# Sampled attention: the last gate weights in slot 5 of the ring, and the queries' copies and two key transposes inside the prompt's attention heads

## The chip, the cores and the metric

The kernel runs on one core of a Trainium2 chip. A core has TensorE (matrix products, PE), VectorE (DVE), ScalarE (ACT), GpSimd (POOL) and SyncE (SP), which issues most of the transfers; 16 DMA engines move the data. The engines run side by side and wait for one another through semaphores. The metric is the device time of one execution in microseconds; lower is better.

## The reference, cut to what matters

It is one layer of a hybrid decoder for a prompt of 256 tokens and 8 sampled sequences of 4 tokens, all float32. One input projection feeds two token mixers, a gated linear attention (branch A) and a softmax attention with a forget bias (branch B, called FoX, 8 heads of 128), and the branch gates. A mixture of experts follows.

```python
qa, ka, va, ra, lra, qb, kb, vb, fb, ga, gb = jnp.split(h @ w_in, offs, axis=-1)
# prompt: causal attention per head, logit[t,s] += F_t - F_s
s = jnp.einsum('bqhd,bkhd->bhqk', qi, k).astype(jnp.float32) * scale
s = s + fi[..., None] - Ft[:, :, None, :]
# samples: 8 pages of 128 keys per sequence, found through page_table, plus the new tokens
k_past = cache_k[page_table].reshape(DB, -1, H, Dh)
v_past = cache_v[page_table].reshape(DB, -1, H, Dh)
s_past = jnp.einsum('bqhd,bkhd->bhqk', q, k_past).astype(jnp.float32) * scale
# both branches meet through the gates
merged = jax.nn.sigmoid(ga) * u_a + jax.nn.sigmoid(gb) * u_b
```

## The kernel before

There are 288 tokens (256 of the prompt, 32 sampled), kept as columns. All weights and cache pages pass through a ring of six slots of 2 MB (`slot(0)` to `slot(5)`). Every engine has its own program, written by hand in one order, and what sets the order between engines is semaphores: `ring_free{s}` says that slot s may be filled, `ring_full{s}` or `kv_full{s}` that it is filled. Each engine and each queue works strictly in the order of its program, so a wait holds everything that stands behind it.

**The gates.** The gate projection (`ga`, `gb`) is used as filling for TensorE. `gates(count)` in the TensorE program does the next `count` steps of it: one step is one product of a 128x128 block of weights with the 288 tokens, and 16 steps make one gate block j. In the trace a float32 product leaves two records, so two steps are four. There are 24 blocks before the sampled attention. Their weights come in 12 loads of 2 MB, load m for blocks 2m and 2m+1, into slots 0 and 1 in turn; ScalarE copies each finished block to a buffer, and the queue of SP stores it (`store_gate`). Eight more blocks follow later, one per sampled sequence (`late_gate`).

**The prompt's heads.** The loop over i from 0 to 8 does, in turn i, the scores of head i and then the weighing of head i-1: TensorE scores, VectorE adds the mask (L1380) and takes the maxima (L1705), ScalarE exponentiates, VectorE inverts the sums (L1712) and scales the probabilities, TensorE transposes them (L642), VectorE copies, TensorE multiplies with the values, VectorE copies the result. TensorE does `gates(5)` behind the scores of a head and `gates(2)` behind the transposes; turn 8 has only the weighing of head 7, with `gates(2)`. With these, the 384th step (the end of block 23) is the last one of turn 8.

**Between the heads and the sampled attention.** After the heads TensorE scores the new tokens (16 pairs of small products). VectorE masks them (L1380), clears `o_all` (L1746), takes the minimum (L1748), and spreads the queries `qb` over the partitions into `q4` by sixteen copies of 32x256. The K pages of a sequence fill slots 0 (pages 0 to 3) and 1 (pages 4 to 7), its V pages slots 2 and 3. VectorE turns keys in blocks of 32x32 (`turn_keys`, L1736) out of slots 0 and 1 into `kT`. That tile lies in slots 4 and 5: heads 0 to 3 (g = 0) in slot 4, heads 4 to 7 (g = 1) in slot 5. Four transposes make one sequence: g = 0 from slot 0, g = 0 from slot 1, g = 1 from slot 0, g = 1 from slot 1; each of the last two frees its slot for the next sequence. `score(b)` on TensorE needs the first two for its first half and all four for its second.

**Who holds slots 4 and 5.** Until then they are the working memory of branch A (`wk`). Its last reader is GpSimd, which multiplies the output of branch A by its norm (L574), its gain (L576) and, all of it at once, by the output gate (L578), and then signals `oa_final`. Just ahead of these it issues the stores of the new K and V (L565 to L570), and just behind them the loads of the forget sums `r_rep` (L585).

Of the kernel before, what the change touches and what calls it, by code (L numbers as in the profile page):

```python
# [17 lines left out]
P = 128  # L18
D = 2048
KT = D // P  # L20
TP = 256
DB, DT = 8, 4
TS = DB * DT
T = TP + TS
# [48 lines left out]
def build(nc, io, out):  # L73
    with ExitStack() as ctx:
# [208 lines left out]
        def place(n):  # L283

            later = LATER if n >= UP and n % SLOTS < 2 else 0
            return n // SLOTS - (1 if n % SLOTS < 2 else 0) + later
# [20 lines left out]
        def later_place(m):  # L307

            return place(UP + m % 2) - LATER + m // 2
# [5 lines left out]
        def _(sp):  # L315
# [45 lines left out]
            for m in range(12):  # L361
                sp.wait_ge(sem(f"ring_free{m % 2}"), later_place(m) + 1)
                at = (COL_GA, COL_GB)[m // 8] + m % 8 * 256
                sp.dma_start(slot(m % 2).rearrange("p (k n) -> p k n", k=KT),
                             io["w_in"][0, :, at:at + 256].rearrange("(k p) n -> p k n", p=P)).then_inc(sem(f"ring_full{m % 2}"), 16)
                if m >= 2:
                    store_gate(2 * m - 4)
                    store_gate(2 * m - 3)
            def gates_back(g):
# [24 lines left out]
            pages(0, 3, lead(3))  # L394
            store_gate(20)
# [4 lines left out]
            pages(0, 1)  # L400
# [229 lines left out]
        def _(pe):  # L630
# [112 lines left out]
            def gates(count):  # L743

                for _ in range(count):
                    j, k = divmod(len(blocks_done), KT)
                    m = j // 2
                    if k == 0:
                        if j % 2 == 0:
                            pe.wait_ge(sem(f"ring_full{m % 2}"), 16 * (later_place(m) + 1))  # L750
                        if j >= 2:
                            pe.wait_ge(sem("gate_copied"), j - 1)
                    w = slot(m % 2).rearrange("p (k n) -> p k n", k=KT)[:, k, j % 2 * P:(j % 2 + 1) * P]
                    last = mm(ps[:, 7 - j % 2, 0:T], w, hT[:, k, :], k == 0, k == KT - 1)
                    blocks_done.append(last)
                    if k == KT - 1:
                        last.then_inc(sem("gate_tile"), 1)
                        if j % 2 == 1:
                            release("gate_tile", j + 1, m % 2)
# [247 lines left out]
            pe.wait_ge(sem("q4_ready"), 1)  # L1007
# [370 lines left out]
        def _(v):  # L1378
# [316 lines left out]
            v.sem_inc(reach("f_ready"), 1)  # L1695
            for i in range(H_B + 1):
                if i < H_B:
# [29 lines left out]
            v.wait_ge(sem("kv_stored"), 6 * 16)  # L1727
# [13 lines left out]
            v.wait_ge(sem("oa_final"), 1)  # L1741
            turn_keys(0, 0, 1, False)
# [3 lines left out]
            nc.vector.memset(o_all, 0.0)  # L1746
# [4 lines left out]

            for part in range(4):
                for a in range(4):
                    last = copy(q4[32 * a:32 * a + 32, :, part, :], qb[32 * part:32 * part + 32, :, TP:T])
            last.then_inc(sem("q4_ready"), 1)
# [30 lines left out]
            turn_keys(0, 1, 4, False)  # L1786
# [275 lines left out]
```

## Time and profile before

| | |
|---|---|
| timed runs | 1976.27, 1983.96, 1987.64 us; median 1983.96 |
| the profiled execution | 1982.53 us, of which the span from the first to the last instruction is 1980.7 |
| TensorE | 1790.8 us busy, 90% of the span |
| VectorE, ScalarE, GpSimd | 531.5, 209.3, 158.5 us busy |
| DMA | 530.86 MB, 268 GB/s over the span |
| granted TensorE clock | 0.953 of full speed on average |

In rows of the profile, L632 and L642 are the two helpers through which all products and transposes of TensorE go, L1380 to L1389 those of VectorE, L1202 that of ScalarE; the tiles tell which work it is. `ring` is a slot or something kept in one, `hT` the tokens, `z`, `work` and `xT` large working tiles, `ps` the result banks of TensorE. "x4" counts records. In square brackets stands how long the engine had been idle before the row, and what ended it. SPq is the queue of SP with its DMA issues. Times are microseconds from the start of the span.

### The profile page before, as it was taken

The page shows a single profiled execution, that of the slowest core. Times are in us where ns is not written, and L with a number is a line of the kernel's source. Part 1 is how long each engine was busy: PE and PEld are TensorE (multiplying, and loading weights), DVE is VectorE, ACT ScalarE, POOL GpSimd, SP SyncE. Part 2 cuts the span into 40 slices and gives each one's busy share as a digit, 9 for nine tenths or more (in the row PEclk, how much of TensorE's full clock was granted, in tenths as well). Part 3 has the DMA queues.
Part 4 walks back from the last instruction along what each step waited for, and adds up shares of the span by engine and source line. Part 5 has one row for each costly group of instructions (what it writes and reads, how often), then busy time and mean ns, then how long its engine had stood idle before and what let it go on. Part 6 is the DMA issues. An engine that isn't in the chain of part 4 may idle for free.

```text
span 1980.7 us, 28087 instructions
## 1 busy us (share of the span) xinstructions
PE 1790.8 (90%) x11118; PEld 1121.3 (57%) x11118; DVE 531.5 (27%) x1145; ACT 209.3 (11%) x403; POOL 158.5 (8%) x274
## 2 busy tenths in 40 slices
PE   6589999999998999997888999998699898999998
PEld 3145666666666786775766777775333333333334
DVE  2020000000008654436555111002423222232223
ACT  2010000000001110211222100002210001000102
POOL 1011011110201000240000000000100000000000
PEclk9789999999999999998989999999799898998999
DMA  9997766685814433747999883333399999999991
GB/s 357 422 351 289 255 256 251 222 322 180 295 46 140 145 98 108 237 154 243 392 391 359 330 294 138 103 117 139 122 359 408 401 392 386 406 384 396 388 399 48
DMA packets 150459, 530.86 MB, mean 268 GB/s; under 512 B 17702, under 2 KB 61900, under 8 KB 123612
## 3 DMA queue, kind: packets, MB, share of 16 engines
q1 hardware_dynamic: 124980, 432.32, 57.6%
q0 software_dynamic: 17088, 97.15, 14.0%
q10 hardware_dynamic: 8336, 0.66, 0.3%
q8 instruction: 36, 0.59, 0.1%
q14 instruction: 19, 0.15, 0.0%
HBM read 510.94 MB, written 19.15 MB: 268 GB/s over the span
## 4 chain that ended last, share of the span: by engine, by line
PE 75%; DMA 12%; DVE 5%; issue 3%; SPq 3%; DVEq 1%; ACT 1%; POOLq 0%; POOL 0%; ACTq 0%
PE ps L632 73%; DMA ring<-in_w_up_e_dram 4%; DMA xT<-in_w_ada_dram 3%; DMA ring<-in_w_ada_dram 3%; PE ps L642 2%; DMA xT<-in_w_in_dram 1%; SPq L384 1%; SPq L378 1%; DVE z L1389 1%; DVE ring L1386 1%; DVE z L1380 1%; DMA z<-in_x_sample_dram 0%; DVEq L2012 0%; DVE ring L1476 0%; DVE ring L1380 0%
## 5 line engine op out<-in xcount | busy, mean ns | idle before, releaser
L632 PE MATMUL ps<-hT,ring 128*128 128x288 f32 x2304 | 585.7, 411 | 9.5 <-ACT hT L1202 6.0
L632 PEld LDWEIGHTS ps<-hT,ring 128*128 128x128 f32 x2304 | 433.1, 191 | 167.7 <-issue 55.3
L632 PE MATMUL ps<-ring,work 128*64 128x512 f32 (+1 forms) x1280 | 281.6, 642 | 36.1 <-DMA ring<-in_w_ada_dram 24.7
L632 PE MATMUL ps<-z,ring 128*128 128x288 f32 (+1 forms) x1040 | 257.5, 408 | 4.5 <-PE ps L632 2.7
L1389 DVE COPY z<-ps 128x256 f32<-128x256 f32 (+7 forms) x98 | 64.3, 659 | 689.8 <-PE ps L632 669.0
L632 PE MATMUL ps<-ring,z 32*32 32x256 f32 (+3 forms) x3744 | 217.2, 400 | 25.8 <-DVE z L1389 11.1
L632 PEld LDWEIGHTS ps<-z,ring 128*128 128x128 f32 x1040 | 197.8, 191 | 62.3 <-issue 6.1
L632 PEld LDWEIGHTS ps<-ring,work 128*64 128x64 f32 (+1 forms) x1280 | 78.3, 136 | 205.1 <-issue 165.6
L632 PEld LDWEIGHTS ps<-ring,z 32*32 32x32 f32 (+3 forms) x3744 | 108.9, 115 | 122.5 <-issue 115.4
L1202 ACT ACTIVATE z<-ps 128x512 f32<-128x512 f32 (+4 forms) x108 | 60.4, 601 | 922.0 <-PE ps L632 910.1
L1386 DVE SCALAR_TENSOR_TENSOR xT<-ps,modT,xT 128x256 f32<-128x256 f32 x160 | 70.8, 480 | 263.6 <-PE ps L632 263.6
L642 PE MATMUL ps<-ident,z 64*128 64x64 f32 (+4 forms) x644 | 92.6, 289 | 42.1 <-DVE z L1380 28.0
L642 PEld LDWEIGHTS ps<-ident,z 64*128 64x128 f32 (+4 forms) x644 | 76.8, 179 | 65.4 <-issue 47.2
L632 PE MATMUL ps<-z 128*128 128x288 f32 (+3 forms) x408 | 109.8, 394 | 2.5 <-DVEq L2023 1.5
L632 PEld LDWEIGHTS ps<-z 128*128 128x128 f32 (+1 forms) x408 | 64.5, 188 | 71.0 <-DVEq L1993 46.1
L632 PE MATMUL ps<-hT,xT 128*128 128x288 f32 (+1 forms) x352 | 84.8, 402 | 19.2 <-DMA xT<-in_w_in_dram 19.2
L632 PEld LDWEIGHTS ps<-hT,xT 128*128 128x128 f32 (+1 forms) x352 | 64.3, 199 | 39.3 <-DMA xT<-in_w_in_dram 20.9
L632 PE MATMUL ps<-xT,work 128*32 128x512 f32 x512 | 67.3, 617 | 13.0 <-DMA xT<-in_w_ada_dram 13.0
L1736 DVE STREAM_TRANSPOSE ring<-ring 128x2048 f32<-128x2048 f32 x32 | 72.2, 2291 | 5.4 <-issue 3.7
L1202 ACT ACTIVATE work<-ps 128x512 f32<-128x512 f32 (+2 forms) x73 | 35.5, 510 | 354.8 <-PE ps L632 306.3
L522 POOL DMA_DIRECT2D xT<-in_w_ada_dram x64 | 34.5, 538 | 319.5 <-PE ps L632 292.2
L608 POOL COPY rstd<-rstd 64x1 int32 (+1 forms) x17 | 3.2, 187 | 472.9 <-PE ps L642 463.4
(201 smaller groups left out, 822.4 us busy)
## 6 DMA issues: line engine op xcount, KB each, us to landing
ring<-in_w_in_dram SPq DMA_DIRECT2D x36, 2048.0 KB, 12.8
xT<-in_w_ada_dram POOLq DMA_DIRECT2D x64, 1024.0 KB, 7.2
ring<-in_w_gate_e_dram SPq DMA_DIRECT2D x32, 2048.0 KB, 13.4
ring<-in_w_up_e_dram SPq DMA_DIRECT2D x32, 2048.0 KB, 18.7
ring<-in_w_down_e_dram SPq DMA_DIRECT2D x32, 2048.0 KB, 15.4
ring<-in_w_ada_dram SPq DMA_DIRECT2D x16, 2048.0 KB, 26.2
ring<-in_cache_v_dram SPq DMA_DIRECT2D x64, 512.0 KB, 5.9
ring<-in_cache_k_dram SPq DMA_DIRECT2D x64, 512.0 KB, 6.0
```

Source lines behind the costliest of these rows:

```text
L378: pg = sp.value_load(ptab[0:1, ds(b * NPG + (s % 2 * 4 + n), 1)], min_val=0, max_val=io["cache_k"].shape[1] - 1)
L384: sp.dma_start(slot(s)[:, n * 1024:(n + 1) * 1024], io[name][0, ds(pg, 1)].rearrange("a p h d -> (a p) (h d)")).then_inc(sem(f"kv_full{s}" ...
L522: pool.dma_start(late[:, k % 2, :], io["w_ada"][0, k * P:(k + 1) * P, ds(i * D + 2 * D, D)]).then_inc(sem(f"late_full{k % 2}"), 16)
L608: pool.tensor_copy(take, token_i[:, ds(w, 1)])
L632: return nc.tensor.matmul(o, lhsT, rhs, start=start, stop=stop, skip_group_check=free)
L642: return nc.tensor.transpose(o, i, ident[0:n, 0:n])
L1202: return nc.scalar.activation(o, i, func, **kw)
L1380: return nc.vector.tensor_tensor(o, a, b, op)
L1386: return nc.vector.scalar_tensor_tensor(out=o, in0=a, scalar=s, in1=b, op0=op0, op1=op1)
L1389: return nc.vector.tensor_copy(o, a)
L1736: nc.vector.transpose(kT[:, g, 4 * half:4 * half + 4], slot(half).rearrange("p (n g e) -> p n g e", n=4, g=2)[:, :, g]).then_inc(sem("keys ...
```

## The change

Three things change, and no arithmetic among them.

1. The last load of gate weights (m = 11, for blocks 22 and 23) goes to slot 5 instead of slot 1, with a semaphore of its own, `last_gates_full`. It waits for `oa_final`. The second half of the first keys, `pages(0, 1)`, is issued ahead of it.
2. VectorE spreads the queries in turns 5 and 6 of the prompt's heads, and does the first two key transposes in turns 7 and 8. What stood behind the heads loses the sixteen copies and two of the four transposes.
3. Before its last two transposes, which write slot 5, VectorE waits until all 24 gate blocks are done; `o_all` is cleared ahead of the new tokens' mask.

```diff
-            later = LATER if n >= UP and n % SLOTS < 2 else 0
+            later = LATER - n % SLOTS if n >= UP and n % SLOTS < 2 else 0
...
-            for m in range(12):
+            def gate_columns(m):
+                at = (COL_GA, COL_GB)[m // 8] + m % 8 * 256
+                return io["w_in"][0, :, at:at + 256].rearrange("(k p) n -> p k n", p=P)
+
+            for m in range(11):
                 sp.wait_ge(sem(f"ring_free{m % 2}"), later_place(m) + 1)
...
             pages(0, 2, lead(2))
             pages(0, 3, lead(3))
+            store_gate(18)
+            store_gate(19)
+            pages(0, 1)
+            sp.wait_ge(sem("oa_final"), 1)
+            sp.dma_start(slot(5).rearrange("p (k n) -> p k n", k=KT), gate_columns(11)).then_inc(sem("last_gates_full"), 16)
             store_gate(20)
             store_gate(21)
             pages(0, 0)
             store_gate(22)
             store_gate(23)
-            pages(0, 1)
             pages(1, 0)
             pages(1, 1)
...
                     if k == 0:
-                        if j % 2 == 0:
+                        if j == 22:
+                            pe.wait_ge(sem("last_gates_full"), 16)
+                        elif j % 2 == 0:
                             pe.wait_ge(sem(f"ring_full{m % 2}"), 16 * (later_place(m) + 1))
...
-            pe.wait_ge(sem("q4_ready"), 1)
+            pe.wait_ge(sem("q4_ready"), 2)
...
+            def spread_queries(*parts):
+
+                for part in parts:
+                    for a in range(4):
+                        last = copy(q4[32 * a:32 * a + 32, :, part, :], qb[32 * part:32 * part + 32, :, TP:T])
+                last.then_inc(sem("q4_ready"), 1)
+
+            def first_keys(half):
+
+                v.wait_ge(sem(f"kv_full{half}"), 64)
+                nc.vector.transpose(kT[:, 0, 4 * half:4 * half + 4], slot(half).rearrange("p (n g e) -> p n g e", n=4, g=2)[:, :, 0]).then_inc(sem("keys_turned"), 1)
+
             for i in range(H_B + 1):
+                if i == 5:
+                    v.wait_ge(sem("kv_stored"), 6 * 16)
+                    spread_queries(0, 1)
+                if i == 6:
+                    spread_queries(2, 3)
+                if i == 7:
+                    v.wait_ge(sem("oa_final"), 1)
+                    first_keys(1)
+                if i == 8:
+                    first_keys(0)
...
-            v.wait_ge(sem("oa_final"), 1)
-            turn_keys(0, 0, 1, False)
+            nc.vector.memset(o_all, 0.0)
...
-            turn_keys(0, 1, 4, False)
+            v.wait_ge(sem("gate_tile"), 24)
+            turn_keys(0, 2, 4, False)
```

The queue of SP, at the last load of gate weights, before (L364 is a load of gate weights, L359 the stores of gate blocks, L378 and L384 the V pages of the first sequence):

```order
L364 DMA ring<-in_w_in_dram 128x16x256 [waits ring_free1]
L359 DMA gates_kept<-work 128x288 [waits gate_copied] x2
L378 TENSOR_LOAD ptab
L378 ISA x2
L384 ISA [waits ring_free2,dve_step]
L384 DMA ring<-in_cache_v_dram 128x1024
```

And of the change (L402 is now the last load of gate weights, L387 the pages):

```order
L387 DMA ring<-in_cache_k_dram 128x1024
L402 DMA ring<-in_w_in_dram 128x16x256 [waits oa_final]
L359 DMA gates_kept<-work 128x288 [waits gate_copied] x2
L381 TENSOR_LOAD ptab
L381 ISA x2
L387 ISA [waits ring_free0]
L387 DMA ring<-in_cache_k_dram 128x1024
```

The load has moved behind eight V pages, two stores and the four K pages of slot 1, and it waits for GpSimd instead of TensorE; the stores of blocks 20 and 21 and the K pages of slot 0 now stand behind that wait.

TensorE in turn 3 of the prompt's heads, where block 22 begins, before (a transpose of head 2's probabilities, the gate steps, the product with the values, the scores of head 4):

```order
L642 MATMUL ps<-ident,z 128x128 [waits gate_tile,fox_pt,fox_prob]
L642 MATMUL ps<-ident,z 128x128 x2
L632 MATMUL ps<-hT,ring 128x288 [waits gate_copied,ring_full1]
L632 MATMUL ps<-hT,ring 128x288
L632 MATMUL ps<-z 128x128 [waits fox_out,fox_pt]
```

And of the change:

```order
L649 MATMUL ps<-ident,z 128x128 [waits gate_tile,fox_pt,fox_prob]
L649 MATMUL ps<-ident,z 128x128 x2
L639 MATMUL ps<-hT,ring 128x288 [waits gate_copied,last_gates_full]
L639 MATMUL ps<-hT,ring 128x288
L639 MATMUL ps<-z 128x128 [waits fox_out,fox_pt]
```

Nothing moves on TensorE; the first gate step of block 22 waits for the new semaphore, and everything behind it on TensorE stands in line.

VectorE from the last copy of turn 7 to the first copies of the forget sums, before:

```order
L1389 COPY z<-ps 128x256
L1712 RECIPROCAL z<-z 128x2
L1383 TENSOR_SCALAR z<-z 128x128
L1383 TENSOR_SCALAR z<-z 128x256
L1389 COPY z<-ps 128x384
L1389 COPY z<-ps 128x256
L1736 STREAM_TRANSPOSE ring<-ring 128x2048
L1380 TENSOR_TENSOR xT<-ps,new_mask 128x2x32
L1746 MEMSET z 128x256
L1748 TENSOR_REDUCE z<-xT 128x2
L1389 COPY z<-z 32x8x32 x16
L1736 STREAM_TRANSPOSE ring<-ring 128x2048 x3
```

And of the change:

```order
L1398 COPY z<-ps 128x256
L1715 STREAM_TRANSPOSE ring<-ring 128x2048
L1743 RECIPROCAL z<-z 128x2
L1392 TENSOR_SCALAR z<-z 128x128
L1392 TENSOR_SCALAR z<-z 128x256
L1398 COPY z<-ps 128x384
L1398 COPY z<-ps 128x256
L1771 MEMSET z 128x256
L1389 TENSOR_TENSOR xT<-ps,new_mask 128x2x32
L1776 TENSOR_REDUCE z<-xT 128x2
L1766 STREAM_TRANSPOSE ring<-ring 128x2048 x2
```

One transpose now stands ahead of the reciprocal of turn 8, the sixteen copies are gone from here, and two transposes follow the new tokens' minimum where three did. In turns 5, 6 and 7 eight copies, eight copies and one transpose stand in the same place ahead of the mask of the turn's head.

## Rows read from the trace of the kernel before

**Rows 1.** The page: busy time by engine, and the chain's shares.

```profile
PE 1790.8 (90%) x11118; PEld 1121.3 (57%) x11118; DVE 531.5 (27%) x1145; ACT 209.3 (11%) x403; POOL 158.5 (8%) x274
...
PE 75%; DMA 12%; DVE 5%; issue 3%; SPq 3%; DVEq 1%; ACT 1%; POOLq 0%; POOL 0%; ACTq 0%
```

**Rows 2.** Timeline from 870 us: start, length, engine, line, operation.

```profile
887.98 0.55 PE L642 MATMUL ps<-ident,z 128*128 128x128 f32 x3 [1.24 <-DVEq L1717]
...
888.37 1.14 PE L632 MATMUL ps<-hT,ring 128*128 128x288 f32 x4
...
889.54 0.41 ACT L1202 ACTIVATE work<-ps 128x288 f32<-128x288 f32 x1 [5.01 <-PE ps L632]
...
891.09 2.30 DVE L1736 STREAM_TRANSPOSE ring<-ring 128x2048 f32<-128x2048 f32 x1
...
893.87 0.24 PE L632 MATMUL ps<-fT,ident 8*32 8x32 f32 x2
...
894.37 0.27 DVE L1746 MEMSET z<- 128x256 f32 x1
...
895.06 4.76 DVE L1389 COPY z<-z 32x256 f32<-32x256 f32 x16
900.29 6.96 DVE L1736 STREAM_TRANSPOSE ring<-ring 128x2048 f32<-128x2048 f32 x3 [0.47 <-DMA ring<-in_cache_k_dram]
...
902.74 7.48 PE L632 MATMUL ps<-ring,z 32*32 32x256 f32 x241 [8.64 <-DVE ring L1736]
```

**Rows 3.** Timeline of the queue of SP, from 800 us.

```profile
826.50 0.39 SPq L364 DMA_DIRECT2D ring<-in_w_in_dram  x1
...
830.51 10.79 SPq L384 DMA_DIRECT2D ring<-in_cache_v_dram  x8
...
891.08 21.89 SPq L384 DMA_DIRECT2D ring<-in_cache_k_dram  x12
913.08 0.40 SPq L391 DMA_DIRECT2D xT<-in_w_in_dram  x1
```

**Rows 4.** Stretches: busy time by engine, granted TensorE clock, DMA share, GB/s.

```profile
894.00:903.00 9.00, 0.36 (x18) 0.29 (x32) 7.98 (x21) 0.00 (x0) 0.00 (x0) 0.51 0.55 174
903.00:908.00 5.00, 4.86 (x160) 2.93 (x134) 4.71 (x3) 0.00 (x0) 0.00 (x0) 0.51 0.38 115
908.00:914.00 6.00, 3.31 (x147) 2.03 (x119) 0.84 (x3) 0.00 (x0) 0.00 (x0) 1.00 0.93 334
922.00:926.00 4.00, 4.00 (x18) 3.40 (x17) 4.00 (x2) 2.15 (x5) 0.00 (x0) 0.63 0.03 9
930.00:960.00 30.00, 29.25 (x797) 23.28 (x799) 14.46 (x16) 6.61 (x18) 1.13 (x2) 1.00 1.03 380
```

**Rows 5.** Timeline of GpSimd, from 826 us.

```profile
831.91 0.80 POOL L574 TENSOR_TENSOR z<-z,ring 128x288 f32<-128x288 f32 x1
842.20 1.01 POOL L576 TENSOR_SCALAR z<-z,vcol 128x288 f32<-128x288 f32 x1 [9.49 <-issue]
...
857.04 5.05 POOL L578 TENSOR_TENSOR z<-z,ring 128x2304 f32<-128x2304 f32 x1
862.70 4.31 POOL L585 DMA_DIRECT2D xT<-r_rows  x8 [0.61 <-issue]
```

**Rows 6.** Timeline from 826 us: TensorE in turn 3, VectorE in turn 4.

```profile
856.28 1.14 PE L632 MATMUL ps<-hT,ring 128*128 128x288 f32 x4
...
860.67 0.43 DVE L1380 TENSOR_TENSOR ps<-ps,fox_mask 128x256 f32<-128x256 f32 x1 [2.12 <-PE ps L632]
```

**Rows 7.** Issue to landing: L364's twelve; those of 804 and 825; V's store.

```profile
DMA to landing us min/median/max: 8.1/9.0/24.1
...
ring<-in_w_in_dram SPq DMA_DIRECT2D x1, 2048.0 KB, 8.3
...
ring<-in_w_in_dram SPq DMA_DIRECT2D x1, 2048.0 KB, 14.8
...
out_v_prompt_dram<-z POOLq DMA_DIRECT2D x1, 1024.0 KB, 10.9
```

More of the change, by code:

```diff
@@ L307, in later_place @@
         def later_place(m):
-            return place(UP + m % 2) - LATER + m // 2
+            return place(UP + m % 2) - (LATER - m % 2) + m // 2
         block = ctx.enter_context(nc.Block())
@@ L359, in store_gate @@
                 sp.dma_start(gates_kept[:, j * T:(j + 1) * T], stage[j % 3]).then_inc(sem(f"gate_kept{j % 3}"), 16)
-            for m in range(12):
+            def gate_columns(m):
+                at = (COL_GA, COL_GB)[m // 8] + m % 8 * 256
+                return io["w_in"][0, :, at:at + 256].rearrange("(k p) n -> p k n", p=P)
+            for m in range(11):
                 sp.wait_ge(sem(f"ring_free{m % 2}"), later_place(m) + 1)
-                at = (COL_GA, COL_GB)[m // 8] + m % 8 * 256
-                sp.dma_start(slot(m % 2).rearrange("p (k n) -> p k n", k=KT),
-                             io["w_in"][0, :, at:at + 256].rearrange("(k p) n -> p k n", p=P)).then_inc(sem(f"ring_full{m % 2}"), 16)
+                sp.dma_start(slot(m % 2).rearrange("p (k n) -> p k n", k=KT), gate_columns(m)).then_inc(sem(f"ring_full{m % 2}"), 16)
                 if m >= 2:
@@ L752, in gates @@
                             pe.wait_ge(sem("gate_copied"), j - 1)
-                    w = slot(m % 2).rearrange("p (k n) -> p k n", k=KT)[:, k, j % 2 * P:(j % 2 + 1) * P]
+                    w = slot(m % 2 if m < 11 else 5).rearrange("p (k n) -> p k n", k=KT)[:, k, j % 2 * P:(j % 2 + 1) * P]
                     last = mm(ps[:, 7 - j % 2, 0:T], w, hT[:, k, :], k == 0, k == KT - 1)
@@ L757, in gates @@
                         last.then_inc(sem("gate_tile"), 1)
-                        if j % 2 == 1:
+                        if j % 2 == 1 and m < 11:
                             release("gate_tile", j + 1, m % 2)
@@ L1724, in _ @@
                     copy(obT[:, h, 0:TP], ps[:, 4 + h % 2, 0:TP]).then_inc(sem("fox_out"), 1)
-            v.wait_ge(sem("kv_stored"), 6 * 16)
             def turn_keys(b, first=0, last=4, again=True):
@@ L1745, in _ @@
                new_mask[:, :].unsqueeze(1).to_broadcast([P, 2, TS]), ALU.add)
-            nc.vector.memset(o_all, 0.0)
             v.drain()
@@ L1750, in _ @@
             v.sem_inc(reach("s_new_copied"), 1)
[L1752 to L1755, printed above, removed]
             def find_max(b):
```

## The prediction

> **What bounds the kernel now.** I read the page first. TensorE is busy for 90% of the span and makes up 75% of the chain that ended last [rows 1], so around the change the question is which wait TensorE has and what ends it. Then I read the timeline of the prompt's attention heads (830 to 891 us) and of the first sampled sequence (891 to 930 us), which is where the diff works.
>
> In the heads TensorE has next to no idle time: the gate matmuls fill it. Behind them comes one long gap. The last gate weights stand in slot 1 until the last gate tile is done at 889.5 us (the matmuls at 888.37 run 1.14 us, and ScalarE's copy starts at 889.54) [rows 2]. Only then does the sync queue issue the second half of the first keys, at 891.08 [rows 3]. VectorE works through one transpose, mask, memset, minimum, sixteen copies (4.76 us) and three transposes (6.96 us), and TensorE's first scores start at 902.74, after 8.64 us of idle time [rows 2]. From there the K and V pages keep the DMA engines at 1.03 of their share between 930 and 960 us [rows 4]: in the loop over sequences a time at which a slot comes free sets the pace, and the whole stream shifts with its first release.
>
> **The term that decides: where the last weights can land.** The new slot, 5, lies in the memory that GpSimd reads until oa_final. GpSimd's last multiplication starts at 857.04 and takes 5.05 us, so oa_final comes at 862.1 [rows 5]. Before, these weights were issued at 826.50 [rows 3]; now the queue may not issue them before 862.1.
>
> When does TensorE want them? The last gate block ends with the two steps of turn 8 (the row at 888.37). Counting back 32 steps of blocks 22 and 23: 2 in turn 8, 7 in each of turns 7, 6, 5 and 4, and 2 in turn 3. So block 22 starts with the two steps (four matmul records) of turn 3, at 856.28 [rows 6]; the order of TensorE shows the new wait at that place. Before oa_final is even reached, TensorE stands.
>
> What the transfer takes: an equal load of gate weights at 804.75 landed after 8.3 us, and the shortest of the twelve took 8.1 [rows 7]. Now GpSimd issues eight loads of 128 KB at 862.70 [rows 5], half as much again. Lower bound 8.1, as if these cost nothing; upper bound 1.5 x 8.3 = 12.4, as if all went ahead (the one load that shared with the K and V stores of 826.50 took 14.8 [rows 7], with far more beside it). I take 10.3, the middle, since the eight loads are spread over 4.31 us. The queue's reaction I put at 0.2 (the distance from the end of GpSimd's last multiplication to its next issue is 0.61 [rows 5]).
>
> A rule to weigh against the row: the Trainium skill, "DMA: Bandwidth & Descriptors", section "Anatomy of one DMA", fits one transfer by 2.0 us plus the bytes at 436 GB/s. That would be 6.8 us for 2 MB, an estimate, where the row has 8.3; by the rule the sum below would be 1.5 us less. I go by the row.
>
> So the stall is 862.1 + 0.2 + 10.3 - 856.3 = **16.3 us**. Behind TensorE's wait stand head 2's product with the values and all that follows; VectorE and ScalarE wait for it, and no other work covers it. Could oa_final come earlier? Between the first multiplication (831.91) and the next GpSimd instruction (842.20) lie 9.49 us that no engine explains [rows 5]. GpSimd's stores of K and V, issued just before, land in that time (the values' 10.9 us after 828.85) [rows 7]. It may be that the drain there waits for them. The weights of 826.50 shared the DMA engines with them and are now gone, but the V pages move up into that place, from 830.51 to about 828.3, since the queue now reaches them directly. Bounds for the change of oa_final: 9.5 us earlier (the wait gone) and 4 us later. I take none.
>
> **After the stall.** The granted clock was 0.51 in the gap of 894 to 903 us, still 0.51 from 903 to 908 with TensorE at work, and 1.00 from 908 on [rows 4]: 5.2 us of work at 1.2 GHz instead of 2.4. After the new stall I charge the same: half of 5.2 = **2.6 us** (bounds 0 and 5.2). By the Trainium skill, "TensorE: Matmul & The Clock Gate", section "HAM oscillation", throttled time costs half of itself when the engine would otherwise be busy; this trace agrees in the level. The old gap's cold stretch ended before the second half of the first scores had its keys (the three transposes end at 907.25), so I credit nothing for it.
>
> **What is put into the heads.** Eight copies are 4.76 / 2 = 2.4 us, one transpose 6.96 / 3 = 2.3 us [rows 2]. They stand where VectorE idled 2.12 us before the mask of the next head [rows 6]: 0.3 too much in each of turns 5 and 6, 0.2 in turn 7, and TensorE has hardly any slack behind it. In turn 8 there is no next head: VectorE goes on to the reciprocal without a wait, and TensorE already waits 1.24 us for it [rows 2], so the transpose costs its whole 2.3. Together 0.3 + 0.3 + 0.2 + 2.3 = **3.1 us** (bounds 2.3, if turns 5 to 7 have slack, and 9.4, if the idle time covers nothing of 2.4 + 2.4 + 2.3 + 2.3). K's halves are there in time: slot 1's pages can go right behind the V pages (about 840 to 850), and slot 0's wait behind the store of block 21, whose copy by ScalarE comes after head 4 and so after the stall, at about 882; they land before 895 and are wanted at about 907. The same queue holds those stores and all later pages behind its wait for oa_final, without harm for that reason. The wait for kv_stored has long been met in turn 5: the values' store lands at 839.8, with only small ones behind it.
>
> **What is taken out behind the heads.** Measured from the end of TensorE's new-token matmuls (894.1): 0.27 memset, 4.76 copies, 0.47 wait for the pages, and one transpose 2.3, since two follow now and not three [rows 2]. The transpose at 891.09 was hidden under TensorE's matmuls and gives nothing. Sum **7.8 us**. Pages of the second sequence, the late gate weights (issued at 913.08 [rows 3]) and the scores all move up by this amount: the scores' second half waits for the last transpose now as before.
>
> **The sum.** 16.3 + 2.6 + 3.1 - 7.8 = **+14.2 us**. The durations are those of one execution of 1982.53 us with a span of 1980.7; the median of the three timed runs is 1983.96, 1.4 higher. Span about 1994.9, that execution 1996.7, and on the median **1998 us**, 0.7% slower. A measurement of this kernel can tell about 0.5%, 9.9 us, from no change.
>
> **The rivals.**
> - *The forecast* (0.71): stall of 14 to 18 us, 1995 to 2001 us on the median from that alone.
> - *GpSimd starts sooner* (0.13). The 9.5 us belonged to DMA traffic that the weights of 826.50 made worse, and it shrinks or goes. For it: the stores land just as it ends. Against it: V pages take the weights' place with twice their bytes. If all goes, the stall is 16.3 - 9.5 = 6.8 and the sum 4.7: 1989 us.
> - *Faster* (0.06): the weights land in time and only the gain is left, 7.8 - 3.1 = 4.7 us, 1979 us. Its one mechanism is oa_final well ahead of block 22. The sign turns when stall and cold clock together are below 4.7, which means weights landed by about 858.5 and oa_final by 848. GpSimd's multiplications from 842.20 to 862.1 take 19.9 us by themselves [rows 5], so even without the wait of 9.5 it is not reached; it needs them shorter too.
> - *Worse* (0.10): the transfer takes the 14.8 us of the contended row, and TensorE's 3.5 us of idle time in turn 8 (1.24 + 2.3) makes the clock fall a second time, as only 0.63 was granted from 922 to 926 in the middle of work [rows 4]: 14.2 + 4.5 + 2, 2005 us.
>
> **How the numbers follow.** Likeliest 1998. The low end takes in most of the second rival, 1988; the high end the fourth and a little, 2007. Its own range without rivals is 1993 to 2003. Slower by over 0.5% means above 1993.9: most of the forecast and the fourth, 0.75. Within 0.5%: the second and the forecast's low edge, 0.19. Faster by over 0.5% would need below 1974; even the third rival gives only 1979, but the timed runs spread from 1976 to 1988, so 0.06.
>
> **What the changed profile should show.** TensorE idle about 16 us at the first gate matmul of turn 3, released by the load into slot 5; that load issued at about 862 and landed after about 10; the granted clock near 0.5 for some 5 us behind it; TensorE waiting about 3.5 us in turn 8; the first scores within 1.5 us of the new-token matmuls instead of 8.64. The prediction is wrong if oa_final comes near 850, or if the clock and the loop behind it don't move with the heads.

## The result and the profile after

The changed kernel takes 1994.39 us (median of ten runs, 1992.00 to 2004.35) against 1981.87 us for the kernel before (ten runs, 1976.27 to 1987.64): a ratio of 1.0073, with an interval of 1.0059 to 1.0088. It is slower by more than the 0.5%, 9.9 us, that the prediction took a measurement here to tell. Its profiled execution has a span of 1992.8 us, 12.1 more than before.

The page of the changed kernel, busy time by engine and the chain's shares (answers to [rows 1]):

```profile
PE 1791.9 (90%) x11118; PEld 1123.4 (56%) x11118; DVE 531.6 (27%) x1145; ACT 209.7 (11%) x403; POOL 159.8 (8%) x274
...
PE 71%; DMA 15%; DVE 4%; issue 3%; SPq 3%; DVEq 1%; POOLq 1%; ACT 1%; POOL 1%; ACTq 0%
```

No engine has more than 1.3 us of additional work. The chain has moved from TensorE (75% to 71%) to DMA (12% to 15%): a wait, not work, was added. Where it stands, the timeline of TensorE and VectorE shows (start, length, engine, line, operation; answers to [rows 2]):

```profile
860.32 0.52 PE L649 MATMUL ps<-ident,z 128*128 128x128 f32 x3 [0.30 <-PE ps L639]
...
878.56 2.29 PE L639 MATMUL ps<-hT,ring 128*128 128x288 f32 x4 [17.73 <-DMA ring<-in_w_in_dram]
...
887.35 1.14 PE L639 MATMUL ps<-hT,ring 128*128 128x288 f32 x4
...
908.83 1.14 PE L639 MATMUL ps<-hT,ring 128*128 128x288 f32 x4
...
911.01 2.30 DVE L1715 STREAM_TRANSPOSE ring<-ring 128x2048 f32<-128x2048 f32 x1
...
914.07 0.55 PE L649 MATMUL ps<-ident,z 128*128 128x128 f32 x3 [3.44 <-DVEq L1748]
914.45 1.14 PE L639 MATMUL ps<-hT,ring 128*128 128x288 f32 x4
...
919.78 0.23 DVE L1389 TENSOR_TENSOR xT<-ps,new_mask 128x64 f32<-128x64 f32 x1 [2.79 <-PE ps L639]
...
920.42 4.77 DVE L1766 STREAM_TRANSPOSE ring<-ring 128x2048 f32<-128x2048 f32 x2
...
920.77 11.28 PE L639 MATMUL ps<-ring,z 32*32 32x256 f32 x368 [1.03 <-DVEq L1777]
```

TensorE stands for 17.73 us at the first step of block 22. Behind the heads the first scores follow at once (1.03 us of idle time instead of 8.64). The chain that ended last, in order of time, shows what made up the wait:

```profile
862.30 5.12 POOLq L586
867.45 11.07 DMA ring<-in_w_in_dram
878.56 8.62 PE ps L639 x32
```

GpSimd's last multiplication ends and releases the sync queue at 867.45. TensorE had been idle since 860.84 (860.32 + 0.52), so 6.6 us of the wait are for GpSimd and 11.1 for the transfer. GpSimd (answers to [rows 5]) still waits about ten microseconds behind its first multiplication:

```profile
836.53 0.81 POOL L581 TENSOR_TENSOR z<-z,ring 128x288 f32<-128x288 f32 x1
847.42 1.02 POOL L583 TENSOR_SCALAR z<-z,vcol 128x288 f32<-128x288 f32 x1 [10.08 <-issue]
...
862.34 5.03 POOL L585 TENSOR_TENSOR z<-z,ring 128x2304 f32<-128x2304 f32 x1
```

The sync queue (answers to [rows 3]) gives the place from which I compare executions, the load of the gate weights for blocks 20 and 21:

```profile
809.37 0.39 SPq L367 DMA_DIRECT2D ring<-in_w_in_dram  x1
...
848.00 4.09 SPq L387 DMA_DIRECT2D ring<-in_cache_k_dram  x4
...
867.45 0.39 SPq L402 DMA_DIRECT2D ring<-in_w_in_dram  x1
...
888.12 4.02 SPq L387 DMA_DIRECT2D ring<-in_cache_k_dram  x4
...
931.05 0.46 SPq L394 DMA_DIRECT2D xT<-in_w_in_dram  x1
```

This load stands at 804.75 us in the trace before and at 809.37 here, so 4.6 us of the difference of the spans lie ahead of anything that the change touches. Whether they belong to the execution or to the kernel isn't shown: the load stands between 805.18 and 813.81 us in all eight traces with the new slot, and between 803.72 and 804.88 in the three without it, though up to there no instruction differs in what it does. All comparisons of traces below count from this load and leave that stretch out. The stretches around the stall and the first scores (busy time by engine, granted clock, DMA share, GB/s; answers to [rows 4]):

```profile
872.00:878.00 6.00, 0.00 (x0) 0.00 (x0) 0.00 (x0) 0.00 (x0) 0.30 (x1) 0.50 1.03 365
...
880.00:882.00 2.00, 2.00 (x10) 1.71 (x9) 0.00 (x0) 0.00 (x0) 0.00 (x0) 0.56 0.00 0
882.00:884.00 2.00, 2.00 (x12) 1.37 (x11) 0.42 (x1) 0.00 (x0) 0.00 (x0) 1.00 0.00 0
...
921.00:925.00 4.00, 4.00 (x128) 2.48 (x105) 3.85 (x2) 0.00 (x0) 0.00 (x0) 0.50 0.21 63
```

The clock was at its low level, 1.2 GHz, in the stall and for some 3.3 us of work behind it, then full. It was low again in the first scores, as it was before the change.

The balance from the trace, counted from that load:
- the stall, 17.7;
- the low clock behind it, 1.7: from block 22 to the same place a head later TensorE takes 8.79 us (878.56 to 887.35) and later 7.13 (887.35 to 894.48, one head and its gate steps at full clock);
- turn 8, 2.2: from its predecessor's gate matmuls to its own 5.62 us (908.83 to 914.45) against 3.44 before (884.93 to 888.37), while turns 5 to 7 together take 21.48 us (887.35 to 908.83) against 21.51 (863.42 to 884.93);
- smaller pieces, -0.6. The mask of the new tokens is then 21.0 us later;
- behind the heads, -7.7: from that mask to the end of the last transpose of the first keys, 13.1 us before and 5.4 after (919.78 to 925.19).

This makes 13.3 at the place where the late gate weights are issued (931.05, against 913.08 in [rows 3]). At the first maximum behind the scores the trace is 10.6 later: another 2.7 us are gained inside the first scores, where TensorE of the kernel before paused without a releaser (timeline of TensorE of the kernel before):

```profile
912.92 3.86 PE L632 MATMUL ps<-ring,z 32*32 32x256 f32 x127 [2.69 <-issue]
```

The DMA views point to what the pause is. One packet of the queue that they call *instruction* (36 packets and 0.59 MB in the whole execution, so 16 KB each) starts at 910.5 us in the trace before, and TensorE goes on 2.4 us behind it. The pause stands in four traces (before, and three of the runs below: the queries alone, oa_final first in the kernel before, the multiplication in eight slices). In each of them this packet starts 7.3 to 8.0 us behind the first score, and TensorE goes on 2.4 to 2.6 us behind it. In the changed kernel it starts 5.1 us behind the first score (925.8), while TensorE still has work, and there is no pause. So TensorE seems to have waited for its next instructions; what sets the moment of the packet isn't shown.

11.1 us are left at the load of the first up-projection's weights, and the medians differ by 12.5. From that load to the end the changed kernel's trace is 3.7 us shorter than the one before (898.7 against 902.4), and the eight traces with the new slot spread there from 898.7 to 905.6. So totals and traces need not agree to a microsecond.

The ten times fall into two groups, six from 1992.0 to 1994.5 and four from 2001.2 to 2004.4. The mean granted clock of the four is 0.945 to 0.949, of the six 0.948 to 0.956; the trace is of one of the six, and no trace shows where the others lose their time.

### The profile page after: what moved, and what is told of

Its sections match the earlier page's. It is cut to its first block, busy times and chain, and to the rows that moved or that the text cites. A ratio compares the mean times of both kernels' runs of the same rounds, so it can differ in the third digit from the quotient of the medians.

```text
span 1992.8 us, 28107 instructions
## 1 busy us (share of the span) xinstructions
PE 1791.9 (90%) x11118; PEld 1123.4 (56%) x11118; DVE 531.6 (27%) x1145; ACT 209.7 (11%) x403; POOL 159.8 (8%) x274
## 4 chain that ended last, share of the span: by engine, by line
PE 71%; DMA 15%; DVE 4%; issue 3%; SPq 3%; DVEq 1%; POOLq 1%; ACT 1%; POOL 1%; ACTq 0%
PE ps L639 69%; DMA ring<-in_w_up_e_dram 6%; DMA xT<-in_w_ada_dram 3%; DMA ring<-in_w_ada_dram 3%; PE ps L649 2%; DMA xT<-in_w_in_dram 2%; SPq L387 1%; SPq L381 1%; DVE z L1398 1%; DVE ring L1395 1%; DMA ring<-in_w_in_dram 1%; DVE z L1389 0%; DMA z<-in_x_sample_dram 0%; POOLq L582 0%; DVE ring L1485 0%
## 5 line engine op out<-in xcount | busy, mean ns | idle before, releaser
L639 PE MATMUL ps<-hT,ring 128*128 128x288 f32 x2304 | 590.6, 414 | 29.1 <-DMA ring<-in_w_in_dram 17.7
L639 PEld LDWEIGHTS ps<-hT,ring 128*128 128x128 f32 x2304 | 435.7, 192 | 189.6 <-issue 57.4
L1766 DVE STREAM_TRANSPOSE ring<-ring 128x2048 f32<-128x2048 f32 x30 | 67.8, 2294 | 6.0 <-issue 3.7
## 6 DMA issues: line engine op xcount, KB each, us to landing
ring<-in_w_in_dram SPq DMA_DIRECT2D x36, 2048.0 KB, 12.5
```

The source lines that it names most:

```text
L639: return nc.tensor.matmul(o, lhsT, rhs, start=start, stop=stop, skip_group_check=free)
L1766: nc.vector.transpose(kT[:, g, 4 * half:4 * half + 4], slot(half).rearrange("p (n g e) -> p n g e", n=4, g=2)[:, :, g]).then_inc(sem("keys ...
```

## The experiments

**Theory A** is the prediction's: the stall in front of block 22 loses the time, it consists of oa_final and the transfer, and what is moved into the heads costs about 2 to 3 us, all in turn 8. **Rival B:** what was put into the heads, and the pages moved ahead of the stores, cost more than that, and the stall less. **Rival C:** the low clock behind the stall is the larger part. Below, "net" is the distance of a place from the load of blocks 20 and 21, less the same distance in the kernel before.

### The slot alone

The new slot stays. Queries are spread and keys turned behind the heads again.

```diff
-                if i == 5:
-                    v.wait_ge(sem("kv_stored"), 6 * 16)
-                    spread_queries(0, 1)
...
-                if i == 7:
-                    v.wait_ge(sem("oa_final"), 1)
-                    first_keys(1)
-                if i == 8:
-                    first_keys(0)
...
+            turn_keys(0, 0, 1, False)
...
+            spread_queries(0, 1)
+            spread_queries(2, 3)
...
-            turn_keys(0, 2, 4, False)
+            turn_keys(0, 1, 4, False)
```

> The change with VectorE's part undone: the last gate weights go to slot 5 behind oa_final and the K pages of slot 1 go early, but the queries' copies and the first two key transposes stand behind the heads as before. Theory (the wait for the weights is the loss): TensorE idles 17 to 18 us in turn 3 and loses about 2 to the low clock, and behind the heads only the 0.47 us wait for pages goes; 18 to 20 us over before, some 7 more than the whole change. Rival (VectorE's work put into the heads is the loss): near before, within 5 us.

Measured: 1999.30 us, ratio 1.0085 (1.0070 to 1.0101). The median is 17.5 us above that of the kernel before and 4.9 above the changed kernel's, not the 7 that I expected. The profiled execution was the slowest of the seven (2008.54), so its trace shows more than the median does: net +23.5 us at the new tokens' mask and +23.1 at the late gate weights. All of the loss is there without any work in the heads, which rules out that part of B; the pages still stand ahead of the stores here. In the trace it is 9.8 more than in the changed kernel: 5.1 for the missing gain (7.7, less the 0.4 that stays, less the 2.2 of turn 8), and 4.6 for the clock. The timeline of TensorE behind the stall:

```profile
880.40 2.29 PE L639 MATMUL ps<-hT,ring 128*128 128x288 f32 x4 [17.82 <-DMA ring<-in_w_in_dram]
...
888.62 5.04 PE L639 MATMUL ps<-hT,ring 128*128 128x288 f32 x10
```

And its stretches:

```profile
886.00:888.00 2.00, 2.00 (x5) 1.16 (x4) 0.00 (x0) 0.00 (x0) 0.00 (x0) 0.50 0.00 0
...
892.00:894.00 2.00, 2.00 (x8) 1.41 (x8) 0.00 (x0) 0.00 (x0) 0.00 (x0) 0.65 0.55 172
894.00:896.00 2.00, 2.00 (x14) 1.64 (x14) 0.89 (x2) 0.00 (x0) 0.00 (x0) 1.00 0.82 246
```

The stall is the same to 0.1 us, but the clock stayed low some 12.6 us, not 3.3: the ten gate matmuls took 5.04 us here and 2.69 in the changed kernel. From block 22 to the same place a head later it is 13.4 us (880.40 to 893.82), 6.3 above 7.13. So the low clock cost 6.3 us in one execution and 1.7 in the other, with the same program up to there. In the trace of *turn 8 without a transpose*, below, nearly the same stall (17.64) was followed by 3.2 us of it. C is not borne out: the clock is the smaller part in both, but the less certain one.

### The queries alone

The kernel before, with the queries' copies in turns 5 and 6 and nothing else.

```diff
+                if i == 5:
+                    v.wait_ge(sem("kv_stored"), 6 * 16)
+                    spread_queries(0, 1)
+                if i == 6:
+                    spread_queries(2, 3)
```

> Before, with only the sixteen copies of the queries moved into turns 5 and 6. Theory (behind the heads the K pages of slot 1, landed at about 900.3, would end the wait anyway): no change, within 1 us of before, and VectorE waits about 5 us for those pages instead of copying. Rival (each microsecond taken from VectorE behind the heads is won): 4.8 us faster.

Measured: 1978.88 us, ratio 0.9987 (0.9973 to 1.0001), no change that can be told. The mask comes net +0.1, the first scores -0.1. The transposes behind the heads show why:

```profile
900.34 6.96 DVE L1747 STREAM_TRANSPOSE ring<-ring 128x2048 f32<-128x2048 f32 x3 [5.20 <-DMA ring<-in_cache_k_dram]
```

VectorE waits 5.20 us for the keys' second half, where it had copied for 4.76 and waited 0.47 [rows 2]. In the heads the copies cost 0.1 us; moved alone they bring nothing, because the transfer that they lay beside ends last. They are worth something only together with the new slot.

### oa_final first, in the changed kernel

GpSimd does its multiplications ahead of the stores of K and V, and the last weights are loaded ahead of the V pages.

```diff
-            pool.wait_ge(*step("kv_tok_ready"))
-            pool.dma_start(out["k_prompt"][0, 0].rearrange("(c p) h d -> p c (h d)", p=P), kbTok).then_inc(sem("kv_stored"), 16)
...
             pool.tensor_tensor(oaT, oaT, sig8, ALU.mult)
...
+            pool.wait_ge(*step("kv_tok_ready"))
+            pool.dma_start(out["k_prompt"][0, 0].rearrange("(c p) h d -> p c (h d)", p=P), kbTok).then_inc(sem("kv_stored"), 16)
...
+            sp.wait_ge(sem("oa_final"), 1)
+            sp.dma_start(slot(5).rearrange("p (k n) -> p k n", k=KT), gate_columns(11)).then_inc(sem("last_gates_full"), 16)
...
-            sp.wait_ge(sem("oa_final"), 1)
-            sp.dma_start(slot(5).rearrange("p (k n) -> p k n", k=KT), gate_columns(11)).then_inc(sem("last_gates_full"), 16)
```

> The change, with GpSimd's multiplications of branch A ahead of its stores of K and V, and the last gate weights issued ahead of the V pages. Theory: oa_final comes near 833, the weights land before 850, the stall and its cold clock (17.7 + 1.8) go, and what is left is the gain behind the heads less turn 8: 6 to 9 us faster than before, 1973 to 1976 where before has 1982. Rival (the gain is paid back by the DMA-bound loop over sequences, or V pages now late hold up the first sequence): within 2 us of before or slower.

Measured: 1989.39 us, ratio 1.0036 (1.0019 to 1.0053); the profiled execution was the slowest of the eight (1997.94). The stall in front of block 22 is gone, and with it 8.3 us of the net loss at the late gate weights (+5.0 against +13.3), but the kernel is not the faster one that I had expected from this. The timeline of all engines at about 839 us shows a new wait:

```profile
839.33 5.11 POOL L577 TENSOR_TENSOR z<-z,ring 128x2304 f32<-128x2304 f32 x1
839.62 4.98 DVE L1392 TENSOR_SCALAR z<-fT 8x288 f32<-8x288 f32 x1
...
844.68 0.65 PE L639 MATMUL ps<-z 128*128 128x128 f32 x2 [4.83 <-DVEq L1703]
```

VectorE's negation of an 8 x 288 tile, some 0.3 us elsewhere, takes 4.98 us: it starts 0.29 us after GpSimd's large multiplication and ends 0.16 us behind it. The first head's product waits for it, and behind the 4.83 us of TensorE the clock was low again, for some 10 us; that head took 9.85 us (844.68 to 854.53), where it takes 5.16 at full clock in the trace before (830.64 to 835.80), 4.7 more:

```profile
846.00:850.00 4.00, 4.00 (x10) 2.29 (x9) 0.32 (x1) 0.00 (x0) 4.00 (x8) 0.50 0.96 253
850.00:854.00 4.00, 4.00 (x9) 2.76 (x9) 0.73 (x3) 0.91 (x4) 3.04 (x6) 0.50 1.05 412
```

The negation ends with GpSimd's instruction, as it would if it were held up until then, and not merely slowed. The Trainium skill, "SBUF — State Buffer", section "Who interferes with whom", says that a tensor_scalar of VectorE can use the port pair that it shares with GpSimd, and that whichever comes first holds it for its whole instruction; these two rows agree with it.

The same run answers the question about oa_final. Without stores ahead of it, GpSimd's wait behind its first multiplication is 0.86 us, not 10.08:

```profile
822.63 1.02 POOL L575 TENSOR_SCALAR z<-z,vcol 128x288 f32<-128x288 f32 x1 [0.86 <-issue]
```

So the wait belongs to the stores that GpSimd itself had issued. By the DMA views it ends 0.7 us behind the landing of the last of the six, before (841.5 and 842.20) and in the changed kernel (846.7 and 847.42). It didn't shrink in the changed kernel, where the old weights' transfer beside it was gone and V pages had its place.

### oa_final first, in the kernel before

The same reordering of GpSimd, in the kernel before, with no new slot.

```diff
-            pool.wait_ge(*step("kv_tok_ready"))
...
+            pool.wait_ge(*step("kv_tok_ready"))
```

> Before, with only GpSimd's multiplications of branch A ahead of its stores of K and V, the last one in one piece. Nothing waits for oa_final there until 891 us, so an early one can bring nothing. Theory: GpSimd's 9.5 us without a releaser are gone (the drain had waited for the stores), and VectorE's negation is held up by the 5.1 us multiplication as in oa_first: 4 to 10 us slower than before. Rival (that hold-up came with the new order of transfers): the same as before within 1 us.

Measured: 1990.32 us, ratio 1.0041 (1.0022 to 1.0061), net +9.4 us at the first scores. The timeline of VectorE and TensorE:

```profile
829.55 4.98 DVE L1383 TENSOR_SCALAR z<-fT 8x288 f32<-8x288 f32 x1
...
834.62 0.49 PE L632 MATMUL ps<-z 128*128 128x128 f32 x2 [4.86 <-DVEq L1694]
```

The same 4.98 us without the new slot and its transfers: the hold-up comes from GpSimd's one long instruction. It costs the wait of 4.86 us and 4.5 more by the first scores, and nearly all of the latter is the clock: it stayed low for some 11 us of work behind the wait (0.50 from 838 to 842), and the first head took 9.58 us (834.62 to 844.20) where it took 5.16 before, 4.4 more. Its ten gate matmuls took 5.17 us, not 2.69.

### The long multiplication in eight slices

oa_final first, with the long instruction cut, so that VectorE can come in between two slices.

```diff
-            pool.tensor_tensor(oaT, oaT, sig8, ALU.mult)
+            for n in range(8):
+                pool.tensor_tensor(oaT[:, n, :], oaT[:, n, :], sig8[:, n, :], ALU.mult)
```

> As oa_first, but GpSimd's last multiplication of 128x2304 (5.1 us in one piece) in eight slices of 128x288 (0.8 us each). In oa_first VectorE's negation of 8x288, 0.30 us elsewhere, took 4.98 us and ended 0.2 us behind that multiplication; TensorE idled 4.83 us behind it and worked about 10 us at 1.2 GHz. Theory (an operation of GpSimd in progress holds up a VectorE operation from SBUF to SBUF, and only until it ends): the negation takes at most 1.3 us, TensorE's idle time and the cold stretch go, 5 to 10 us faster than oa_first and 3 to 8 us faster than before. Rival (the negation waits for something else, such as the transfers that start then): it still takes about 5 us, and the kernel stays 5 to 8 us over before.

Measured: 1979.53 us, ratio 0.9984 (0.9969 to 0.9999); net -3.3 us at the late gate weights. The negation takes 0.74 us. Next in the same timeline stand turn 8 and the first scores:

```profile
834.50 0.74 DVE L1393 TENSOR_SCALAR z<-fT 8x288 f32<-8x288 f32 x1
...
894.71 0.90 PE L650 MATMUL ps<-ident,z 128*128 128x128 f32 x3 [3.44 <-DVEq L1749]
...
903.03 7.42 PE L640 MATMUL ps<-ring,z 32*32 32x256 f32 x242 [1.03 <-DVEq L1778]
```

The weights are issued at 840.47 and no stall is left. Seen against the changed kernel (+13.3) this is 16.6 us at the late gate weights, and the times part too (0.9984 against 1.0073). What was changed for it is when the memory of slot 5 comes free and that its load is the first to be issued then. The K pages still stand ahead of the stores here, which speaks against the other part of B. The transpose in turn 8 still costs its wait of 3.44 us, and the clock was low behind it (0.80 and 0.77 in two stretches of 4 us). The time hardly differs from that of the kernel before (2.8 us on the medians, where I had expected 3 to 8), and TensorE pauses inside the first scores again, for 3.01 us behind these 242 matmuls.

### The same, with the keys one turn earlier

```diff
-                if i == 5:
+                if i == 4:
                     v.wait_ge(sem("kv_stored"), 6 * 16)
                     spread_queries(0, 1)
-                if i == 6:
+                if i == 5:
                     spread_queries(2, 3)
-                if i == 7:
+                if i == 6:
                     v.wait_ge(sem("oa_final"), 1)
                     first_keys(1)
-                if i == 8:
+                if i == 7:
                     first_keys(0)
```

> As oa_sliced, with the queries spread in turns 4 and 5 and the first two transposes in turns 6 and 7, so that nothing is put into turn 8. Theory (turn 8 has no idle time to take a transpose, turns 6 and 7 have): TensorE's idle time in turn 8 falls from 3.44 to about 1.24 us, 2 to 4 us faster than oa_sliced, 6 to 11 us faster than before. Rival (the transpose costs the same in any turn): the same as oa_sliced within 1 us.

Measured: 1976.54 us, ratio 0.9972 (0.9953 to 0.9990), the lowest median here and faster than the kernel before, by 0.3% only, 5.7 us on the medians where I had expected 6 to 11. Against the version in eight slices the median is 3.0 us lower, but the intervals overlap. Net -7.4 us at the late gate weights, -7.8 at the up-projection. TensorE in turn 8 and at the first scores:

```profile
893.40 0.55 PE L650 MATMUL ps<-ident,z 128*128 128x128 f32 x3 [1.25 <-DVEq L1749]
...
900.15 11.28 PE L640 MATMUL ps<-ring,z 32*32 32x256 f32 x368 [1.03 <-DVEq L1778]
```

The wait of turn 8 is back to the 1.24 us of before [rows 2], and what the change was worth behind the heads is kept whole.

### Turn 8 without a transpose, in the changed kernel

```diff
-                if i == 8:
-                    first_keys(0)
...
+            first_keys(0)
```

> The change, with the second of the two early transposes moved from turn 8 to behind the heads, where TensorE scores the new tokens. Theory (it is hidden there as in the kernel before): TensorE idles 1.24 instead of 3.44 us in turn 8 and the first scores come as soon behind the new tokens; 2 to 3.5 us faster than the change, 9 to 12 us over before. Rival (it is only moved): the same as the change within 0.5 us.

Measured: 1993.36 us, ratio 1.0058 (1.0037 to 1.0079). In the trace TensorE's wait in turn 8 is 1.25 us again, and the late gate weights come 2.3 us earlier than in the changed kernel (+11.0 against +13.3), the size of one transpose. The ratio is 0.15% below the change's, which the intervals don't part, so the gain in time isn't shown.

### The last weights in four transfers

The load into slot 5 is cut into four, each of four k-blocks, and TensorE waits for each when it needs it.

```diff
-            sp.dma_start(slot(5).rearrange("p (k n) -> p k n", k=KT), gate_columns(11)).then_inc(sem("last_gates_full"), 16)
+            for part in range(4):
+                sp.dma_start(slot(5).rearrange("p (k n) -> p k n", k=KT)[:, 4 * part:4 * part + 4],
+                             gate_columns(11)[:, 4 * part:4 * part + 4]).then_inc(sem(f"last_gates_full{part}"), 16)
...
+                    if j == 22 and k % 4 == 0:
+                        pe.wait_ge(sem(f"last_gates_full{k // 4}"), 16)
```

> The change, with the last gate weights as four transfers of 512 KB, each with its own semaphore, TensorE waiting before each fourth step of block 22 for its part. The two steps of turn 3 need only the first. Theory (of the 17.7 us stall 6.6 are the wait for oa_final and 11.1 the transfer): the first part lands 4 to 7 us after its issue and the stall is 11 to 14 us; 4 to 7 us faster than the change, 8 to 11 us over before. Rival (all parts share the DMA engines with one another and with GpSimd's loads, so that the first lands hardly sooner): within 1 us of the change.

Measured: 1989.79 us, ratio 1.0053 (1.0034 to 1.0072). The stall, in the timeline of TensorE:

```profile
871.01 2.26 PE L641 MATMUL ps<-hT,ring 128*128 128x288 f32 x4 [10.54 <-DMA ring<-in_w_in_dram]
```

It is 7.2 us shorter, and 7.1 of them arrive at the late gate weights (+6.2 against +13.3). TensorE had waited for 2 MB where it needed the first quarter. The median is 4.6 us below the changed kernel's, as expected, but the intervals overlap (1.0053 and 1.0073).

### TensorE kept at work through the stall

44 matmuls on data that is there, whose results nobody reads (two records each), are put in front of the wait, so that TensorE works through it.

```diff
                         if j == 22:
+                            pe.wait_ge(sem("gate_copied"), 21)
+                            for _ in range(44):
+                                mm(ps[:, 7, T:512], ones[:, :], hT[:, 0, 0:512 - T], True, True)
                             pe.wait_ge(sem("last_gates_full"), 16)
```

> The change, with 44 products of 128x224 (results unused, in a free part of a result bank) issued just ahead of the wait for the last gate weights, about 16.4 us of work at full clock, so that TensorE idles only 1 to 2 us. Theory (the low clock behind the stall costs 1.8 us): 1 to 2.5 us faster than the change, and the granted clock stays at 1.00 behind the wait. Rival (the clock costs nothing, as VectorE and ScalarE set the pace of a turn): the same as the change within 0.5 us, with a granted clock of 1.00 as well.

Measured: 1998.71 us, ratio 1.0099 (1.0081 to 1.0117): not faster than the changed kernel, and what I expected of the total is missed. TensorE's timeline and, in a fence of its own, two stretches:

```profile
856.49 16.81 PE L639 MATMUL ps<-hT,ones 128*128 128x224 f32 x88
...
875.05 1.24 PE L639 MATMUL ps<-hT,ring 128*128 128x288 f32 x4 [1.75 <-DMA ring<-in_w_in_dram]
...
909.01 0.90 PE L649 MATMUL ps<-ident,z 128*128 128x128 f32 x3 [3.44 <-DVEq L1751]
```

```profile
856.00:873.00 17.00, 16.86 (x91) 16.85 (x91) 0.56 (x1) 0.00 (x0) 10.98 (x11) 1.00 0.54 183
...
908.00:912.00 4.00, 2.99 (x10) 2.42 (x11) 1.41 (x5) 0.13 (x1) 0.00 (x0) 0.57 0.00 0
```

The clock stayed full through the stall and behind it, and the four gate matmuls take 1.24 us instead of 2.29. The stall itself ended 0.7 us later, counted from the load of blocks 20 and 21 (69.9 against 69.2), since the transfer took 11.9 and not 11.1. But then the clock fell behind the wait of turn 8, which the changed kernel passed at 1.00, and what was won was lost: net +14.0 at the late gate weights, as without the filler (+13.3). One trace can't say whether the filler brought that on, since the clock fell there in the sliced version too, without filler. In this execution the 1.7 us of the low clock behind the stall were not won. At the load of the first up-projection's weights it is +14.3 against +11.1, and the median is 4 us above the changed kernel's, with intervals that overlap; where these few microseconds arise I can't say.

## Why the prediction was right

The prediction named the sign, the place and the mechanism, and its terms stand beside the measured ones, in us:

| term | predicted | measured | shown by |
|---|---|---|---|
| stall in front of block 22 | 16.3 | 17.7 | the changed kernel; the slot alone 17.8 |
| low clock behind it | 2.6 | 1.7, and 6.3 in the slot alone | those two traces |
| work put into the heads | 3.1 | 2.2 in turn 8, 0 to 0.1 in turns 5 to 7; -0.6 in smaller pieces | trace; turn 8 cleared gives 2.3 |
| behind the heads | -7.8 | -7.7 | trace |
| sum at the late gate weights | +14.2 | +13.3 | |
| further gain in the first scores | none | -2.7 | trace; -2.7 in the slot alone too |
| median | 1998, +14 | 1994.4, +12.5 | |

The sum came out closer than its terms: the stall was 1.4 too small, the clock, the heads and the smaller pieces together 2.4 too large, and the missed gain of 2.7 lies behind the place of the sum. That these nearly cancel is luck. The 1998 also stand on a median of three runs before that was 2.1 us above the median of ten.

**The stall.** oa_final came 58.0 us behind the load of blocks 20 and 21, not 57.4, of which 0.6 is GpSimd's wait, 10.08 instead of 9.49; the transfer took 11.1, between the bounds of 8.1 and 12.4, a bit above the middle that I took for it; the 6.8 us that the prediction estimated beside its row were further off. That it is the stall that decides was shown by the sliced version, which frees the memory earlier, loads without a stall, and gives back 16.6 us. The rival *GpSimd starts sooner* fell: its wait didn't shrink without the old weights' transfer. The reordering runs show that it hangs on GpSimd's own stores of K and V, the alternative that the prediction had named and given no move.

**The clock.** Its size was near in the profiled execution (1.7 for 2.6) and is no constant: the same stall was followed by 3.3 us of low clock in one execution and 12.6 in another, which cost 6.3. The bounds of 0 to 5.2 were too narrow for this term.

**The work in the heads.** The 0.3 + 0.3 + 0.2 for turns 5 to 7 were too much. VectorE's copies of 2.35 us push the mask by 0.2 and 0.3 us, the transpose by 0.03, and TensorE takes up all but 0.1 of it. The 2.3 of turn 8 were right.

**What was missed.** Above all, that the 8.64 us of idle time and the pause inside the first scores are separate: the second is gone after the change, and was not in the sum. It goes with the moment of one 16 KB packet of instructions, and not with the work that was moved: it is gone in the slot alone too, it came back in the sliced version (3.01 us), and with the keys one turn earlier it was gone again. What sets that moment stays open.

**What stays open:** the two groups of times of the changed kernel (1992 to 1994 and 2001 to 2004). A low clock of 3 or of 13 us behind the stall is worth some 5 us and could be a part of it, and so could a second fall behind turn 8, which the fourth rival had named and which two other traces show; no run parts them. Open, too, is where the 4.6 us ahead of the change come from.

## What to carry to other kernels

Moving a load to a buffer of its own frees the old one, but the load then starts when the new buffer's last reader is done: put that time beside the time at which the consumer wants the data before anything else, and here the 6.6 us between them and one transfer of 11 us outweighed all that was gained. If such a load can't be issued sooner, cut it, so that the first matmuls wait for a quarter and not for the whole (7.2 us of the wait in one trace). Small work may be put into idle time of an engine where something follows it with slack, but not into the last turn, where its consumer already waits.

## What the runs showed of the hardware

- **GpSimd's wait behind its own stores.** GpSimd's wait after its first multiplication, where its program has a drain, took 9.49 and 10.08 us with the stores of K and V issued just ahead of it, and 0.86 with the stores behind, in both kernels. With the stores ahead it ended 0.7 us behind the landing of the last of them.
- **VectorE held for the length of a GpSimd instruction.** 4.98 us for an operation that takes about 0.3, beside one GpSimd multiplication of 5.11 us, and 0.74 beside eight slices of it.
- **The low clock's length varies.** Behind a stall of 17.7 to 17.8 us of the same program TensorE worked at the low level for 3.3 us in one execution and 12.6 in another; behind waits of 4.83 and 4.86 us it was low for some 10 and 11 us, and the head behind them took 4.7 and 4.4 us longer.
- **The same idle time of 3.44 us in turn 8** was followed by full clock in the changed kernel (1.00 from 914 to 918) and by a low one in two others (0.57 with the filler and 0.77 in the sliced version), so one trace of such a place doesn't give its price.
- **A pause for instructions.** TensorE stood for 2.10 to 3.01 us inside the first scores in the four traces in which a 16 KB packet of the instruction queue started 7.3 to 8.0 us behind the first of them. It went on 2.4 to 2.6 us behind the start of that packet. Where the packet started 5.1 us behind the first score, as in the changed kernel, it didn't stand.
